# Two weight slots loaded ahead, the first v gathers tied to query products 5 to 7, and moved homes of the u rows

## The reference

```
q = (xc @ peer_wq).reshape(TOKEN_CHUNK, PEER_HEADS, PEER_DQ)      # 8 heads of 256
s1 = einsum('chd,nd->chn', q[..., :half], peer_keys[0]); s2 = ...  # 128 keys each
v1, i1 = top_k(s1, 16); v2, i2 = top_k(s2, 16)
top_s, pos = top_k(v1[..., :, None] + v2[..., None, :], 16)        # over 256 pairs
e = expert number of each of the 16;  g = softmax(top_s)
h = gelu(einsum('cd,chkd->chk', xc, peer_u[e]))
out = einsum('chk,chkd->cd', g * h, peer_v[e])
```

## Time and profile before

| | |
|---|---|
| Time, median of 3 runs | 1361.41 us (1357.44 to 1363.77) |
| The profiled execution's own time | 1354.4 us |
| Its span in the profile | 1352.6 us |
| PE busy / DVE / ACT / POOL | 81% / 53% / 31% / 66% |
| Moved by DMA | 356.86 MB, mean 264 GB/s |
| Gathers by POOL's queue | 268.47 MB of it |

### The profile page before, as it was taken

The page is one execution under the profiler, slowest core; times in us unless marked ns, Lnnn a source line. Parts: engine busy times, 40 slices in busy tenths (PEclk is TensorE's granted clock), DMA queues, the critical chain, the costliest instruction groups (busy, mean ns, idle before and its releaser), DMA issues.

```text
span 1352.6 us, 14212 instructions
## 1 busy us (share of the span) xinstructions
PE 1101.4 (81%) x4814; PEld 735.0 (54%) x4814; DVE 714.1 (53%) x1600; ACT 419.0 (31%) x761; POOL 895.2 (66%) x845
## 2 busy tenths in 40 slices
PE   6999999999999998996858757766877776686757
PEld 5778898999988877893313313322333232232322
DVE  6436222222263786594646567746665664572842
ACT  4355454444435445534202202220222022012202
POOL 5764448788897675686565757666766666765670
PEclk9999889999999999997988879768977877887878
DMA  7533225555554312499799999999999999989891
GB/s 253 182 129 121 77 84 187 171 178 179 179 190 179 109 48 100 161 373 350 304 389 350 365 370 366 352 352 408 348 346 360 382 359 350 411 339 366 310 410 65
DMA packets 89442, 356.86 MB, mean 264 GB/s; under 512 B 9648, under 2 KB 9776, under 8 KB 81840
## 3 DMA queue, kind: packets, MB, share of 16 engines
q0 software_dynamic: 73728, 268.47, 51.5%
q1 hardware_dynamic: 15232, 86.15, 17.9%
q10 hardware_dynamic: 432, 1.57, 0.4%
HBM read 355.10 MB, written 1.05 MB: 263 GB/s over the span
## 4 chain that ended last, share of the span: by engine, by line
PE 15%; DVE 12%; issue 10%; another core or an unknown queue 8%; POOL 3%; DMA 1%; ACT 1%; DVEq 0%; ACTq 0%; POOLq 0%
PE bank L1008 14%; DVE u_row L1913 7%; POOL v_row L2036 2%; POOL u_row L2036 2%; DMA v_row<-peer_v_dram,expert 1%; DVE gain L1843 1%; ACT diag L1360 1%; DVE gain L1894 0%; DVE c_part L1895 0%; DVE gain L1892 0%; DVE c_pos L1850 0%; DVE s_idx L1846 0%; DVE s_idx L1850 0%; DVEq L1392 0%
## 5 line engine op out<-in xcount | busy, mean ns | idle before, releaser
L1008 PE MATMUL bank<-v_row,diag 128*128 128x512 f32 x960 | 500.4, 669 | 197.2 <-issue 156.4
L1998 POOL TENSOR_TENSOR w_lo<-raw,w_hi 128x512 fp32r<-128x512 f32 x296 | 375.7, 1303 | 155.4 <-ACT w_hi L1126 155.0
L1008 PEld LDWEIGHTS bank<-v_row,diag 128*128 128x128 f32 x960 | 200.9, 212 | 496.4 <-issue 453.9
L1913 DVE CUSTOM_DVE_ANT_0 u_row<-u_row,bank 128x1024 f32<-128x1024 f32 x256 | 298.5, 1218 | 63.6 <-issue 52.3
L2036 POOL DMA_INDIRECT u_row<-peer_u_dram,expert x256 | 248.7, 972 | 113.5 <-issue 78.3
L2036 POOL DMA_INDIRECT v_row<-peer_v_dram,expert x240 | 226.7, 945 | 138.9 <-issue 67.3
L612 PE MATMUL bank<-hT_hi,w_hi 128*128 128x256 f32 x672 | 194.7, 290 | 5.2 <-issue 1.8
L614 PE MATMUL bank<-hT_hi,w_lo 128*128 128x256 f32 x672 | 192.6, 287 | 5.7 <-issue 5.7
L613 PE MATMUL bank<-hT_lo,w_hi 128*128 128x256 f32 x672 | 192.5, 286 | 2.4 <-issue 2.3
L1126 ACT ACTIVATE w_hi<-raw 128x2048 fp32r<-128x2048 f32 x79 | 150.9, 1911 | 109.0 <-PE bank L614 64.7
L1353 ACT ACTIVATE gelu<-dots 128x16 f32<-128x16 f32 x16 | 3.5, 216 | 476.5 <-DVE dots L1913 221.1
(11 more groups left out here) (259 smaller groups left out, 1333.4 us busy)
## 6 DMA issues: line engine op xcount, KB each, us to landing
raw<-stream_dram SPq DMA_DIRECT2D x79, 1024.0 KB
u_row<-peer_u_dram,expert POOLq DMA_INDIRECT x256
v_row<-peer_v_dram,expert POOLq DMA_INDIRECT x240
residual<-x_in_dram SPq DMA_DIRECT2D x2, 512.0 KB, 4.6
out_dram<-residual SPq DMA_DIRECT2D x4, 256.0 KB, 2.1
consts<-consts_in_dram SPq DMA_DIRECT2D x1, 840.0 KB, 13.5
gain<-norm_final_dram ACTq DMA_DIRECT2D x1, 512.0 KB, 7.5
normed_tokens<-norm_g_dram ACTq DMA_DIRECT2D x1, 512.0 KB, 3.5
```

Source lines behind the costliest of these rows:

```text
L1008: ins = mm(accs[half][:, :], diag[:, 2 * m + i, :], row[:, half * 512:(half + 1) * 512], start=False, stop=True, skip_group_check=True)
L1913: ins = v.tensor_tensor_reduce(out=row_of_u, in0=row_of_u, in1=hn_tile[:, :], scale=1.0, scalar=0.0, op0=ALU.mult, op1=ALU.add, accum_out= ...
L1998: ins = nc.gpsimd.tensor_tensor(w_lo[r][:, cols], raw[r][:, cols], w_hi[r][:, cols].bitcast(F32), ALU.subtract)
```

## The change

Two raw slots are added, `raw_ahead0` and `raw_ahead1`, for the last two granules, wq6 and wq7. They lie at `m0 + 4D` and `m0 + 6D`, where queries and keys of the attentions and 20 of the 28 diagonals of the convolution have been. SP issues both loads right behind that of wq1, after waiting for the last scores of attention "G" and for the convolution's diagonal products. The loop of SP's other loads ends at wq5.

The homes of the rows move. u batches 0 to 3 lie at `m0` to `m0 + 4D` and `m0 + 8D` to `m0 + 12D`, batches 4 to 6 in the three raw slots (the slots of wq3, wq4, wq5 in this order), batch 7 in `raw_ahead0`. So batches 4 to 7 of the first group wait for late splits 1 to 4. v batches 0 and 1 lie in `w_hi` and `w_lo` of wq5, 2 and 3 in those of wq6, 4 and 5 in those of wq7, batch 6 in `raw_ahead1`, batch 7 where it was. The v gathers of the first group wait for query product 5 before batch 0, product 6 before batch 2 and product 7 before batch 4.

```diff
-EARLY_U = 6
+FREE_U = 8
+AHEAD = 2
...
+        ahead_cols = [m0 + 4 * D + i * GRAIN for i in range(AHEAD)]
+        raw += [at(f"raw_ahead{i}", col, [P, GRAIN]) for i, col in enumerate(ahead_cols)]
...
+        ring_slots = [(NGRAN - LATE + i) % RING for i in range(RING)]
+        u_cols = rows_at(m0, m0 + 2 * D, m0 + 8 * D, m0 + 10 * D, *[r * GRAIN for r in ring_slots], ahead_cols[0])
+        hi_lo = [part * RING * GRAIN + (n % RING) * GRAIN for n in range(NGRAN - RING, NGRAN) for part in (1, 2)]
+        v_cols = rows_at(*hi_lo, ahead_cols[1], x0 + 4 * D)
...
+        def raw_slot(n):
+
+            return n % RING if n < NGRAN - AHEAD else RING + n - (NGRAN - AHEAD)
...
-            for n in range(RING, NGRAN):
-                late = n - RING - (NGRAN - LATE)
-                if late < 0:
-                    sp.wait_ge(split_done, n - RING + 1)
-                else:
-                    sp.wait_ge(late_split_done, late + 1)
+            for n in range(RING, NGRAN - AHEAD):
+                sp.wait_ge(split_done, n - RING + 1)
                 load(n)
+                if GRANULES[n] == "wq1":
+                    ps.full(sp, ("taps",))
+                    ps.full(sp, ("scores",) + units("G")[-1])
+                    for ahead in range(NGRAN - AHEAD, NGRAN):
+                        load(ahead)
...
-                if m >= EARLY_U:
-
-                    pool.wait_ge(late_split_done, LATE - RING + 1 + m - EARLY_U)
+                if 2 * m >= FREE_U:
+
+                    pool.wait_ge(late_split_done, m + 1 - FREE_U // 2)
                 fetch_u(0, m, m + 1)
...
-            ps.full(pool, ("query", NH - 1))
             for m in range(BATCHES):
+                if m % 2 == 0 and m // 2 < RING:
+                    ps.full(pool, ("query", NH - RING + m // 2))
                 gather(peer_v, v_rows, v_in, 0, m)
```

18 lines of the change are left out of this document (9 added, 9 removed).

## The result

The changed kernel is slower, by about 1%. Both kernels ran 16 times side by side: 1359.35 us median for the kernel before (1352.32 to 1366.22), 1371.1 us for the changed one (1363.51 to 1380.29); the ratio is 1.0118, with a 95% interval from 1.0096 to 1.014. The forecast was 1353.4 us; the rival called "slower" had said 1370.4. The profiled execution took 1372.21 us with a span of 1370.4, against 1354.4 and 1352.6 before.

What follows compares the result with a forecast made beforehand. Taken as the bound: the chain behind starved query product 7 into the expert loop. Direct terms were 0, the likeliest case gained 8 us: 1361.4 - 8 = 1353.4 us. Range 1347 to 1371 us.

Steps and rivals of the forecast that it cites:

- slower: Rival, chance 0.21: early v gathers prolong product 7's starving until near 633.9, the whole chain +9 us, 1370.4 us.
- What bounds the kernel: Way into the expert loop: product 7 loses 12.5 us, delaying gate, dots, third choice and POOL's u gather at 653.31.
- Starved of instructions: PE in product 7, from 610.27: it lacks instructions while gathers fill the DMA engines; 12.5 us lost.
- Part 1, loads ahead: SP's last two loads behind wq1's: direct cost and gain 0; 2.1 MB leave the gathers' ramp, full from 600, not 585.
- the loads disturb the projection: Rival, chance 0.04: PE starved near 530 to 536 in the output projection, nothing else gained, +1 to +2 us, 1363.
- Part 2, homes: First group's u batches wait for late splits that are done before their gathers' turn; POOL gains and loses 0.
- The sum's key step: PE runs dry 24 us after DMA engines fill; full only from 600, that falls at 624, so product 7 ends at 611.1.
- The whole 8 us gain: Likeliest case, chance 0.50: product 7 starves less and the expert loop starts 8 us earlier, between 5.1 and 12.5.
- Part 3: First v gathers after products 5, 6, 7: start at 618.93, 5.2 us sooner, end at 638.5; alone that buys nothing.
- I let a shift at its start reach its end.: Expert loop: fourteen more groups repeat their waits, so the 8 us won at the start was carried whole to the end.

Runs made afterwards that it cites:

- f2: The changed kernel with all first v gathers waiting for query product 7 again, on a starving chip: 1360.81 us, ratio 1.0005 to the kernel before.
- h1: The changed kernel, POOL waiting for product 7 before the second group's u batch 4, first v gathers behind that; starving chip: 1361.16 us, ratio 0.9987.
- i3: The kernel before with 127 further instructions at the head of PE's program, on a starving chip: 1376.52 us, ratio 1.0167.
- e1: The changed kernel with all first v gathers waiting for query product 7 again, on a quiet chip: 1251.77 us, ratio 1.000 to the kernel before.
- h3: The changed kernel, unedited, on a starving chip: 1374.08 us, ratio 1.0065 to the kernel before.
- g3: The kernel before, each u batch from the second group on waiting until u rows two batches earlier have landed; quiet chip: 1259.16 us, ratio 1.0057.
- g4: The kernel before with 127 further instructions at the head of PE's program, on a quiet chip: 1260.67 us, ratio 1.0068.
- e3: The changed kernel with late loads and first v gathers behind product 7, leaving only new homes and slots; quiet chip: 1253.47 us, ratio 1.0021.
- f1: The changed kernel, unedited, on a starving chip: 1370.61 us, ratio 1.0062 to the kernel before.
- i1: The changed kernel with the last two weights loaded late again, early v gathers kept; starving chip: 1379.39 us, ratio 1.0178 to the kernel before.
- i2: The kernel before, each u batch from the second group on waiting until the batch just ahead has landed; starving chip: 1518.31 us, ratio 1.1222.
- j1: The kernel before with one gap per group from the second on, before u batch 4; quiet chip: 1299.56 us, ratio 1.0384.
- j2: The kernel before with two gaps per group from the second on, before u batches 3 and 6; quiet chip: 1344.68 us, ratio 1.0758.

## Why the prediction was wrong, step by step

- **What bounds the kernel.** The chain through product 7 into the third group was read rightly; in the changed kernel, f2 and h1 the gate follows product 7 (in the changed kernel and in h1 it stands 2.7 us behind the last of its scores, as before). "Starved of instructions" was not borne out: the same program with equally full DMA engines does not starve on a quiet chip, a shift by 127 instructions leaves the dry point in product 7, and PE crawls while no instruction packet is on its way. I had held the trace against the rule of the Trainium skill (Runtime: NRT & Kernel Launch, instruction fetch mechanics) that fetching is mostly hidden, and had taken the trace to speak against it; the packet rows and i3 agree with the rule.
- **Part 1, loads ahead.** (The two loads moved up four places in SP's order; "six" above was a miscount.) Issue without a wait (525.60), the traffic in 525 to 535 and 317 GB/s in the ramp against some 300 expected: right. In the changed kernel's profiled execution the gathers began 1.9 us later than before. PE's granted clock in 525 to 535 was 0.83 there and 1.00 before, so part of the work ahead of the projection ran at the lower level of 1.2 GHz. Whether the loads bring this about is open. e1 and h3, which have them, show the same 0.83, but so does g3, which has not, and six others with the loads show 1.00. The first u gather lies at 568.57 to 574.37 (mean 571.4) in the nine profiles with the loads ahead and at 567.92 to 572.16 (mean 569.9) in the nine without, g4 and i3 left aside. The case "the loads disturb the projection" (+1 to +2 us) is neither shown nor ruled out.
- **Part 2, homes.** Zero or nearly so, as predicted (e1 at 1.000, f2 at 1.0005; e3 at 1.0021).
- **The sum's key step failed.** "With the engines full only from 600, the same delay falls at 624." The ramp did get lighter, and PE went dry at 611.12, 37.7 us behind the first gather, as in the kernel before (37.6 in f2, 39.1 in i3). What counts starts with the gathers, not with full engines. The whole 8 us gain hung on this step. I had taken the delay from one event, without a second one to tell the two readings apart; the stall at 588.82, which comes 16.2 to 16.8 us behind the first gather in every profile from a starving chip, was there and I used it as an argument against.
- **Part 3, and the rival "slower".** With that step gone the condition of the rival was met, and its mechanism came as described, each time within 1.5 us: POOL went on until 630.35 (predicted 628.9), product 7 ended at 633 (predicted 633.9), POOL's third group 7.6 us late (predicted 9), of which 1.9 us came from ahead of the expert layer. f1, f2, h3 and i1 show it as cause, on the starving chips. It had a chance of 0.21 for the reason just named: I believed that the ramp's load decides.
- **"I let a shift at its start reach its end."** This failed too. From the start of the loop to the end the changed kernel lost another 10 us, and the profiled h1 was 8 us early at the third group and level with the kernel before at the fourth. That the rival's 1370.4 came so near the measured 1371.1 is in part luck. Its one term was 9 us on a base of 1361.4. In the profiled executions the start gave 7.6 us and the loop 10; the medians of 16 differ by 11.8, on a base of 1359.35.
- **The range** (1347 to 1371) ended 0.1 us short of the median of 1371.1, because it had no term for the loop.

## What to carry to other kernels

When an engine stalls without a named wait, find out what ends the stall before moving work to where it happens: here a pause of the engine that issues the gathers ended it, and the change filled that pause. Do not carry a shift through a loop that has a bottleneck and a pause of its own; look at which chain stands in the pause, since that sets the period. And measure on more than one chip before tuning against a stall with no name.

## What the runs showed of the hardware that I had not expected

- The same kernel took 1251 to 1254 us on three chips and 1360 to 1366 us on three others, about 9% apart, each chip met once; the mean granted clock of PE in the profiled executions is 0.98 on the former (kernels without added gaps) and 0.89 on the latter, where windows in which PE crawls show its lower level (0.50, 1.2 GHz, in 620 to 630 of the changed kernel).
- On the slower chips PE went nearly dry 37.6 to 39.5 us after the first gather of a stretch without a gap, with the DMA share in the 10 us before at 0.91 or 0.99, and came back within some 5 us of a gap; a pause of 3.62 us was enough to keep product 7 free of all but one stall. The quiet chips, at a DMA share of 1.03, showed nothing of the kind.
- Where the engines starve, the trace loses landing records: 3082 of 9648 are left in the kernel before, 8289 in i2, all on quiet chips.
- A gap made by waiting for the landing of the batch just issued costs 3.3 us where nothing starves (j1, 15 gaps), and two in a group cost nearly twice that (j2).
